# Five preloads of ScalarE's function tables in the RWKV rounds and norms of a hybrid decoder step

## What is computed

```python
def layer_norm(x, g, b):
    mu = jnp.mean(xf, axis=-1, keepdims=True)
    var = jnp.mean(jnp.square(xf - mu), axis=-1, keepdims=True)
    y = (xf - mu) * lax.rsqrt(var + LN_EPS) * g + b
...
def rwkv7_mixer(x, shift0, wkv0, v_first, W, j):
    w = -softplus(-(w0 + tanh(xw @ w1) @ w2)) - 0.5
    a = sigmoid(a0 + (xa @ a1) @ a2)
    g = sigmoid(xg @ g1) @ g2
    kk = heads(k * k_k)
    kk = kk / max(sqrt(sum(kk * kk, -1)), 1e-12)
    k = k * (1.0 + (a - 1.0) * k_a)
    decay = exp(-exp(heads(w)))
    y, s = rwkv7_scan(rh, decay, kh, vh, -kk, kk * ah, wkv0)
    y = head_group_norm(y, lnx_g, lnx_b)
    y = y + sum(rh * kh * r_k, -1) * vh
    out = (y * g) @ w_o
```

## Time and profile before

| | |
|---|---|
| three runs, median | 4374.54 us (4366.42 to 4386.37) |
| the profiled execution | 4375.82 us, its span 4374.1 us |
| TensorE busy | 3874.8 us, 89% of the span |
| VectorE busy | 1625.2 us, 37% |
| ScalarE busy | 1166.4 us, 27% |
| GpSimd busy | 306.0 us, 7% |
| mean granted TensorE clock | 0.945 |

### The profile page before, as it was taken

One profiled execution on the slowest core, in us unless ns is written; L12 is line 12 of the kernel. 1 busy time (PEld: TensorE's weight loads), 2 busy tenths in 40 slices (PEclk: granted clock), 3 DMA queues, 4 the chain that ended last, 5 costly groups with the idle time before them and its releaser, 6 DMA issues.

```text
span 4374.1 us, 84510 instructions
## 1 busy us (share of the span) xinstructions
PE 3874.8 (89%) x36015; PEld 3403.1 (78%) x36015; DVE 1625.2 (37%) x2134; ACT 1166.4 (27%) x1626; POOL 306.0 (7%) x526
## 2 busy tenths in 40 slices
PE   6979797969899999989799877888879899999989
PEld 4646474759799999979499766666659799999979
DVE  2435353533422232352522154545424423232352
ACT  2122223221412121231122244454431412121131
POOL 2120202030000000000300011111100000000000
PEclk9989898989999999999899899899889999999999
DMA  2222212031111111111122201000001111111102
GB/s 82 62 71 56 78 50 77 23 88 39 30 48 43 45 44 44 44 32 37 31 80 80 74 25 43 25 25 25 26 20 35 34 49 39 45 48 44 44 29 72
DMA packets 305296, 206.20 MB, mean 47 GB/s; under 512 B 26280, under 2 KB 290142, under 8 KB 304926
## 3 DMA queue, kind: packets, MB, share of 16 engines
q1 hardware_dynamic: 290174, 161.38, 12.9%
q0 software_dynamic: 11200, 25.97, 2.1%
q10 hardware_dynamic: 3552, 13.41, 0.8%
HBM read 173.66 MB, written 27.04 MB: 46 GB/s over the span
## 4 chain that ended last, share of the span: by engine, by line
PE 75%; DVE 7%; ACT 5%; issue 5%; POOLq 2%; PEld 1%; ACTq 1%; DVEq 1%; PEldq 1%; POOL 0%; DMA 0%; SPq 0%
PE ps L1651 73%; ACT big L644 3%; PEld ps L1651 1%; ACT ring L644 1%; POOLq L313 1%; DVE xa L1339 1%; ACT xa L644 1%; PE ps L2142 1%; DVE big L1440 1%; DVE h_hi L1082 1%; ACTq L751 1%; DVE big L1251 1%; DVE small L1227 1%; DVE big L1082 1%; DVEq L1229 0%
## 5 line engine op out<-in xcount | busy, mean ns | idle before, releaser
L1651 PE MATMUL ps<-h_hi,wparts 128*128 128x364 f32 (+1 forms) x4992 | 1003.1, 331 | 38.7 <-DVE h_lo L1335 20.8
L1651 PEld LDWEIGHTS ps<-h_hi,wparts 128*128 128x128 f32 x4992 | 860.2, 190 | 42.1 <-DVE h_lo L1335 23.5
L1651 PE MATMUL ps<-x_lo,wparts 128*128 128x364 f32 (+1 forms) x3360 | 698.7, 332 | 39.2 <-DVE h_hi L1082 39.2
L1651 PE MATMUL ps<-x_hi,wparts 128*128 128x364 f32 (+1 forms) x3072 | 604.2, 331 | 39.2 <-DVE x_lo L1335 21.4
L1651 PEld LDWEIGHTS ps<-x_lo,wparts 128*128 128x128 f32 x3360 | 582.7, 190 | 44.2 <-issue 32.8
L1651 PEld LDWEIGHTS ps<-x_hi,wparts 128*128 128x128 f32 x3072 | 526.9, 189 | 43.8 <-issue 23.9
L1651 PE MATMUL ps<-h_lo,wparts 128*128 128x364 f32 (+1 forms) x2112 | 468.4, 330 | 0.0
L644 ACT ACTIVATE big<-ps 128x512 f32<-128x512 f32 (+10 forms) x334 | 199.8, 621 | 1006.5 <-PE ps L1651 435.3
L644 ACT ACTIVATE wparts<-ring 128x1024 fp32r<-128x1024 f32 x200 | 200.6, 1004 | 925.9 <-PE ps L1651 906.5
L1651 PE MATMUL ps<-big 64*64 64x64 f32 (+6 forms) x7192 | 326.0, 268 | 98.6 <-DMA big<-in_cache_v 52.4
L1651 PEld LDWEIGHTS ps<-big 64*64 64x64 f32 (+3 forms) x7192 | 257.4, 147 | 171.4 <-issue 103.2
(11 more groups left out here) (229 smaller groups left out, 3359.4 us busy)
## 6 DMA issues: line engine op xcount, KB each, us to landing
ring<-in_mlp_up SPq DMA_DIRECT2D x64, 512.0 KB, 4.0
ring<-in_mlp_down SPq DMA_DIRECT2D x64, 512.0 KB, 3.9
ring<-in_w_in_even SPq DMA_DIRECT2D x28, 512.0 KB, 7.1
rkv_scratch<-big ACTq DMA_DIRECT2D x24, 544.0 KB, 2.7
big<-rkv_scratch SPq DMA_DIRECT2D x24, 544.0 KB, 4.8
big<-in_cache_k SPq DMA_DIRECT2D x128, 64.0 KB, 1.9
big<-in_cache_k POOLq DMA_DIRECT2D x128, 64.0 KB, 2.1
big<-in_cache_v SPq DMA_DIRECT2D x128, 64.0 KB, 1.9
```

What stands on the lines that cost most here:

```text
L1651: return pe.matmul(out, lhsT, rhs, start=start, stop=stop, skip_group_check=True)
```

## The change

Five calls that preload a table set are put into ScalarE's program, in five functions: Ln's set in each norm ahead of the wait for `ln_var`, Sigmoid's ahead of the decay's waits, Ln's behind the rate's Sigmoid, Exp's behind `key_log`, Ln's behind the group norm's Square and Copy. No other engine's program changes.

```diff
@@ norm
                 if n % 2:
                     split_w(stage, 0, 1, 256)
                     act.wait_ge(pt_tr, n)
                     f(xs(pt_hi, 0), pset(0), ACT.Copy).then_inc(xhi_ok, 1)
+                act.preload_act_table(ACT.Ln)
                 act.wait_ge(ln_var, n + 1)
                 rsqrt_mean(ln["RSTD"], pset(1), D, EPS_LN).then_inc(ln_rstd, 1)
@@ decay_in
+                act.preload_act_table(ACT.Sigmoid)
                 act.wait_ge(rw_dve, n * 8 + 1)
                 act.wait_ge(rw_mm, n * 4 + 1)
                 f(w["LW"], bank(5, T), ACT.Sigmoid, bias=cur[:, 0:1]).then_inc(rw_act, 1)
@@ key_log
                 act.wait_ge(rw_dve, n * 8 + 5)
                 f(w["RN"], w["RN"], ACT.Ln)
+                act.preload_act_table(ACT.Exp)
```

## The result

| | before | after |
|---|---|---|
| median of 22 runs each | 4376.67 us | 4390.51 us |
| lowest to highest | 4364.21 to 4386.37 | 4382.9 to 4399.4 |
| ratio, 95% interval | | 1.0032, 1.0024 to 1.0039 |
| the profiled span | 4374.1 us | 4387.9 us |
| mean granted TensorE clock | 0.945 | 0.942 |

The change costs 0.32%, or 14.0 us (10.5 to 17.1). It goes the way that was forecast, and 4390.51 us lies inside the range of 4370 to 4400 us, but the 9.0 us of the forecast were too few. With 22 executions of each kernel the interval is clear of no change, although 0.32% is less than the 0.5% that the prediction took for the limit of such a measurement.

The account below looks back on a forecast made before the run. TensorE holds three quarters of the chain of waits, so ScalarE counts only where another engine waits for it. Terms 1.3 + 10.1 + 1.4 - 1.8 - 2.0 = +9.0 us gave 4384 us, range 4370 to 4400.

Parts of the forecast that it names:

- Ln's preload behind the rate's Sigmoid: Before key_square's Square: Square and key norm 1.44 us late in seven rounds, +10.1 us, and once ahead of the loop, +1.4.
- rival 3: Longer idle before the key norm lowers TensorE's clock: up to 4.8 us a round, up to 4418 us; chance 0.09.
- The scan, -1.8: Exp's load leaves the exponentials' front; VectorE's sum at the fourth step takes back most: -1.8 us, ends 0 and -10.0.
- rival 1: At the scan, VectorE's sum does not hold TensorE, so each round keeps 1.43 us: 4376 us; chance 0.14.
- The group norm, -2.0: Ln's preload behind Square and Copy fits a wait; Ln starts 0.28 us earlier in seven rounds: -2.0 us.
- Norm 0, +1.3, and norms 1 to 3, 0: Norm 0's new Exp load between Ln and Exp is exposed, +1.3 us; in norms 1 to 3 nothing changes.
- Sigmoid's preload and key_log, 0: Before the decay the load already stands beside a wait; at key_log the next copies wait for TensorE anyway: both 0.
- Rivals 2: The late Square is absorbed because another wait of level 3 ends as late as the key norm: 4373 us; chance 0.08.
- 4: Rival 4: nine exposed new loads cost twice, each also waiting for its engine to drain: 11.7 us more, 4396 us; chance 0.03.
- 5: Rival 5: Ln's preload brings the set with both functions, Exp loads go and the norm costs nothing; chance 0.01.
- the longer gap at the scan's fourth step: Expected sign: TensorE waits longer there behind VectorE, while its idle before the first scan copy falls to about 0.6 us.
- the signs that it named against itself: Key-norm idle staying 0.8 us, the scan ending earlier against VectorE's sum, or rounds changing by whole clock falls.

Follow-up runs that it names:

- ln_behind_square: The changed kernel with Ln's preload moved from behind the rate's Sigmoid to behind the keys' Square; ratio 0.9994 to the kernel before.
- norms_only: The kernel before with Ln's preload in the four norms only; ratio 1.0005 to the kernel before.
- rate_only: The kernel before with only Ln's preload directly behind the rate's Sigmoid; ratio 1.0039, 17 us slower than before.
- two_loads_again: The kernel two_loads run once more, in one session with a twin whose gap was filled by matmuls; ratio 1.0078, 34 us slower than before.
- after_again: The changed kernel run once more, in one session with a twin whose gap was filled by matmuls; ratio 1.0042, 18 us slower than before.
- one_set: The kernel before with one preload only, the set holding both Ln and Exp, behind the keys' Square; ratio 0.9983, 7 us faster than before.
- exp_only: The kernel before with Exp's preload behind key_log only; ratio 0.9999 to the kernel before.
- one_set_rows_late: The kernel one_set with two VectorE products for the next pair put behind the sums the scan waits for; ratio 0.9969, 14 us faster than before.
- two_loads: The changed kernel with a second load, Exp's, ahead of Ln's between the rate's Sigmoid and the Square; ratio 1.0086, 38 us slower than before.

## Why the prediction was right, and where its sizes were off

- **Ln's preload behind the rate's Sigmoid, +10.1 and +1.4.** Right to 0.1 us in total: 11.5 us more idle time in the group, and the whole loss goes with this preload's place (ln_behind_square).
- **What the step left out** is the key norm's own duration, which the forecast kept at 2.15 us. It is 9.3 us longer over the seven rounds. This is rival 3, to which a chance of 0.09 was given: its place and cause were right, at 1.3 us a round in place of up to 4.8, because behind the key norm no loss shows in sum (from its end to the copy ahead of the exponentials the seven rounds changed by 0.2 us together, single ones by -1.4 to +2.5). The argument against it, that the 2.07 us before each scan bring no fall, did not carry over to another place. A sign stood in the earlier trace rows: behind 2.25 us of idle the same six matmuls took 4.01 us. It does not decide, since the granted clock was 0.50 ahead of that idle time too (2495.00 to 2503.10), but the prediction used the row for the wait alone.
- **The scan, -1.8.** Mis-sized: from the copy to the sixth step the trace has -4.8 us. Three rounds won 0.24 us each that were put at 0: the 0.15 us of idle before VectorE's sum were a wait for TensorE, as the row's bracket says, and went. The two rounds that were put at 0.97 and 0.74 won 1.43 and 1.65. That VectorE's sum takes back the rest is seen in the new 0.72 us of waiting, and rival 1's 1.43 us in every round did not come. The size is known to some us only: over the seven rounds this stretch takes 71.2 to 72.6 us in the three traces with the load ahead of the exponentials (before, norms_only, rate_only), and 67.4 to 69.9 in eight of the nine with Exp's preload (71.2 in two_loads_again).
- **The group norm, -2.0.** Right: Ln is 0.28 us earlier in each of the seven rounds, 1.99 us in sum.
- **Norm 0, +1.3, and norms 1 to 3, 0.** Right: 6.45 against 5.17 us of waiting in norm 0, hidden in norm 1; in norm 2 the Exp load still stands between Ln and Exp.
- **Sigmoid's preload and key_log, 0.** Right: in the round of the earlier trace rows the decay's Sigmoid waits 0.18 us for TensorE as before, and the copies of level 5 still wait.
- **Rivals 2, 4 and 5** fall. The Square's delay was not absorbed. The added loads take 1283 ns too; the one behind the rate's Sigmoid starts 0.02 us behind it and ends 0.01 us ahead of the Square, so the drain that the Trainium skill has ("ScalarE: Activation LUTs", What ACT_TABLE_LOAD costs) is not in these traces. Each Ln preload was followed by an Exp load.

With the measured sizes the terms give 11.5 + 9.3 + 1.3 - 4.8 - 2.0 = 15.3 us, against 14.0 measured (10.5 to 17.1). The two profiles alone differ by 13.8 us, but 7.5 us of that come behind the last round's `gate`, where no term lies, so their difference is not a proof of the terms.

That the time fell into the range is in part luck. Two errors went against each other, 9.3 us that were left out and 3.0 too little for the scan, and the range had room for one or two falls of the clock at up to 4.8 us each, where six came at 1.1 to 2.0. The idle time before the key norm and the longer gap at the scan's fourth step came as the prediction said; but of the signs that it named against itself, that the rounds change by falls of the clock came true in part.

Left open: how much a second load costs. Its wait (10.4) and the slower key norms (3 to 5) make 13 to 16 us; by the ratios of two sessions it is 24, by the medians of one session (4410.62 for two_loads_again, 4392.25 for after_again) 18. And how much of the time that filling saves at the key norm is lost again in other stretches.

## What to carry to other kernels

The loads that the compiler placed here wait for no semaphore, so they already hide in a wait of the activation behind them; look in the timeline for loads with no idle time behind them, for moving the others gained nothing in these traces. Put a preload behind the instruction that another engine waits for, not in front of it (17 us here), and name a set that serves the next two functions where there is one (one_set, 7 us). When a wait in front of TensorE's matmuls grows, look at the duration of the matmuls behind it as well.

## What the runs showed of the hardware

Behind 0.80 us of idle the six matmuls of the key norm took 2.15 us in 38 of 42 cases: in all 21 of the kernels before, norms_only and ln_behind_square, while exp_only and one_set had one slow case each and one_set_rows_late two (3.76 to 3.85 us). Behind 2.23 us they were slow, 2.93 to 4.10 us, in 17 of 21 cases (the changed kernel twice and rate_only); behind 3.5 us in 14 of 14 (two_loads twice). With the gap filled by unused matmuls they took 2.15 us in 21 of 21. So idle time in front made the slow key norm likely, but four came without the longer gap. At 4.10 us the granted clock was 0.50, the lower level of 1.2 GHz. In the seven rounds 10.0 us of added idle time came with 9.3 us of longer matmuls behind it; whether the price is the same in another place no run here shows. Behind the 2.07 us before the scan of the earlier trace rows the granted clock was 1.00 (2678.00 to 2681.00).
